# Reordering the half steps of an RWKV-7 scan on one core: partial gram mask, kept state on another engine, low-rank products earlier

## The reference

```python
def step(S, inp):
    r_t, w_t, k_t, v_t, a_t, b_t = inp
    sa = jnp.einsum('zdhij,zdhj->zdhi', S, a_t)
    S = S * w_t[..., None, :] + sa[..., :, None] * b_t[..., None, :] + v_t[..., :, None] * k_t[..., None, :]
    y = jnp.einsum('zdhij,zdhj->zdhi', S, r_t)
    return S, y
```

## Time and profile before

| | us |
|---|---|
| median of three runs | 2652.01 |
| lowest, highest | 2651.32, 2657.9 |
| the profiled execution's own time | 2653.14 |
| its span, first to last instruction | 2650.9 |
| granted TensorE clock over the span | 0.977 |

### The profile page before, as it was taken

The page is one execution under the profiler, slowest core; times in us unless marked ns, Lnnn a source line. Parts: engine busy times, 40 slices in busy tenths (PEclk is TensorE's granted clock), DMA queues, the critical chain, the costliest instruction groups (busy, mean ns, idle before and its releaser), DMA issues. The chain is left out here.

```text
span 2650.9 us, 63375 instructions
## 1 busy us (share of the span) xinstructions
PE 2475.4 (93%) x28048; PEld 2055.0 (78%) x28048; DVE 1259.8 (48%) x2464; ACT 686.7 (26%) x1647; POOL 831.4 (31%) x627
## 2 busy tenths in 40 slices
PE   7999999999998688888888879999999999999997
PEld 6785568888887577777777757878888888888886
DVE  3106650000654456666666656554444444444446
ACT  4115651111111344434434433220011100111002
POOL 3322122222331333324233338023233322433234
PEclk9999999999999799989999989999999999999999
DMA  5100011111110000000000034220011101111014
GB/s 162 44 32 18 2 49 72 72 72 68 37 40 22 37 4 4 4 4 4 3 4 4 4 120 183 89 79 32 33 48 41 40 33 44 37 40 40 33 61 146
DMA packets 39085, 123.09 MB, mean 46 GB/s; under 512 B 11425, under 2 KB 11425, under 8 KB 37665
## 3 DMA queue, kind: packets, MB, share of 16 engines
q1 hardware_dynamic: 38816, 119.06, 12.9%
HBM read 96.24 MB, written 20.97 MB: 44 GB/s over the span
## 5 line engine op out<-in xcount | busy, mean ns | idle before, releaser
L2024 DVE TENSOR_TENSOR ff_f<-ff_f,ff_ps 128x512 f32<-128x512 f32 x300 | 205.5, 687 | 173.6 <-PE ff_ps L98 173.6
L2043 DVE TENSOR_TENSOR ff_sq<-ff_rl 128x512 f32<-128x512 f32 (+1 forms) x96 | 122.4, 1275 | 273.1 <-ACT ff_rl L1941 273.0
L1941 ACT ACTIVATE ff_rl<-ff_ps 128x512 f32<-128x512 f32 (+1 forms) x96 | 50.6, 527 | 754.9 <-PE ff_ps L98 754.9
L733 ACT ACTIVATE sc_xy<-sc_ps 128x256 f32<-128x256 f32 x320 | 120.8, 384 | 225.6 <-PE sc_ps L427 224.1
L1810 POOL TENSOR_TENSOR ff_wd0h<-ff_wdr,params 128x1024 fp32r<-128x1024 f32 x16 | 30.3, 1893 | 458.0 <-DMA ff_wdr<-in_w_down 458.0
L427 PE MATMUL sc_ps<-sc_xy,sc_q 64*64 64x64 f32 x3200 | 166.1, 226 | 0.4 <-issue 0.3
L411 PE MATMUL sc_ps<-sc_xy,sc_ai 64*64 64x64 f32 x3200 | 122.9, 239 | 37.5 <-DVE sc_xy L877 31.4
L977 DVE TENSOR_TENSOR sc_q<-sc_ps,sc_cs 128x128 f32<-128x128 f32 x400 | 98.8, 279 | 122.5 <-PE sc_ps L411 118.8
L423 PE MATMUL sc_ps<-sc_q,sc_xy 64*64 64x64 f32 x2560 | 122.2, 241 | 30.1 <-DVE sc_q L977 24.1
L98 PE MATMUL ff_ps<-hh,ff_wu0h 128*128 128x512 f32 (+1 forms) x384 | 136.7, 356 | 4.4 <-issue 4.4
L427 PEld LDWEIGHTS sc_ps<-sc_xy,sc_q 64*64 64x64 f32 x3200 | 137.8, 142 | 0.7 <-issue 0.5
(11 more groups left out here) (304 smaller groups left out, 7174.8 us busy)
## 6 DMA issues: line engine op xcount, KB each, us to landing
ff_wur<-in_w_up SPq DMA_DIRECT2D x32, 512.0 KB, 3.5
ff_wdr<-in_w_down SPq DMA_DIRECT2D x32, 512.0 KB, 4.2
gwr<-in_w_in SPq DMA_DIRECT2D x31, 512.0 KB, 3.2
gm_dram<-gp_gm SPq DMA_DIRECT2D x8, 1280.0 KB, 4.4
ff_m<-gm_dram SPq DMA_DIRECT2D x16, 640.0 KB, 7.7
fr_x<-in_x SPq DMA_DIRECT2D x10, 512.0 KB, 5.1
ff_xs<-in_x SPq DMA_DIRECT2D x10, 512.0 KB, 3.9
x_dram<-ff_xo SPq DMA_DIRECT2D x10, 512.0 KB, 2.9
```

Of the source, the lines that this page charges most:

```text
L733: nc.scalar.activation(XY[g][:, :, :, :].rearrange("p n u t -> p n (u t)"), yx_out[g], ACT.Copy).then_inc(xy_ready, 1)
L1941: nc.scalar.activation(rl[v % 2][:, 0:tn], ps[:, b, 0:tn], ACT.Relu).then_inc(relu, 1)
L2024: nc.vector.tensor_tensor(own, own, ps[:, 4 + v % 4, :], ALU.add).then_inc(added, 1)
L2043: nc.vector.tensor_tensor(sq[v % 2][:, 0:tn], rl[v % 2][:, 0:tn], rl[v % 2][:, 0:tn], ALU.mult).then_inc(squared, 1)
```

## The change

The edit moves and splits instructions in the four streams; the sums are the same.

- `start_group` masks the strict part first (`begin`, now with the 128 columns of it, signalled by `first_ready`), goes on to the transpose, and masks the other 384 columns last (`mask`). `flip` waits for `masked` of both groups, since it writes into the gram's bank.
- `keep` goes from VectorE to ScalarE, as two passes of 64 columns with a pointer scale.
- In odd half steps `lora_products` stand in front of level 1 and `lora_tanh` behind level 0's copies; the wait for `ta_ready` stands at the first gram. `half` is split over levels 1 and 3, and the two scans go from level 0 of the even half step to level 3 of the odd one. `lora_tanh` waits for the scans of the step before and for POOL's last reading of `icl` (`icl_used`), the scans for the end of POOL's step before (`arr_ready`).
- The second gram stands in front of both level 4 products.
- Both square roots and the products that feed them move back, to between levels 3 and 4.

```diff
@@ POOL, prepare @@
-                own.mark(nc.gpsimd.tensor_tensor(k, fac[:, :, :], both_blocks(raw_k, i), ALU.mult))
-                own.wait()
+                nc.gpsimd.tensor_tensor(k, fac[:, :, :], both_blocks(raw_k, i), ALU.mult).then_inc(icl_used, 1)
+                pool.wait_ge(icl_used, q + 1)
@@ TensorE, flip @@
                 pe.wait_ge(x1_ready, q * GR + g + 1)
+                pe.wait_ge(masked, q * GR + g // HALF * HALF + HALF)
@@ TensorE, side, odd half steps with i == 1 @@
-                    if spot == 0 and ct + 1 < CT:
+                    if spot == 2 and ct > 0:
+                        pe.wait_ge(sqy_ready, ct * NG)
+                        by_head(GRAM_BANK, std, var_ps)
+                    if spot == 2 and ct + 1 < CT:
                         pe.wait_ge(sqk_ready, (ct + 2) * NG)
                         by_head(TOK_BANK, nrm, ss_ps)
-                    if spot == 5 and ct > 0:
-                        pe.wait_ge(sqy_ready, ct * NG)
-                        by_head(GRAM_BANK, std, var_ps)
-                    if spot == 6 and ct > 0:
+                    if spot == 3 and ct > 0:
                         pe.wait_ge(std_ready, ct)
-                    if spot == 1 and ct + 1 < CT:
+                    if spot == 4 and ct + 1 < CT:
                         pe.wait_ge(nrm_ready, ct + 2)
@@ TensorE, the half step @@
                 side(t, 0)
+                if ahead:
+                    lora_products(q + 2)
                 if levels:
                     level_q(q, 1, ga)
...
-                side(t, 6)
+                if ahead:
+                    pe.wait_ge(ta_ready, q + 3)
                 if more:
                     gram_products(qa, sa)
...
                 side(t, 2)
-                if ahead:
-                    lora_products(q + 2)
...
-                if levels:
-                    level_xy(q, 4, ga)
                 side(t, 3)
-                if ahead:
-                    pe.wait_ge(ta_ready, q + 3)
                 if more:
                     gram_products(qa, sb_)
                 if levels:
+                    level_xy(q, 4, ga)
                     level_xy(q, 4, gb)
@@ ScalarE @@
                     if q:
-                        act.wait_ge(arr_ready, q)
+                        act.wait_ge(cum_ready, 2 * q)
+                elif q:
+                    act.wait_ge(icl_used, q)
...
+            def keep(q, g):
+                i, n = q % NB, q * GR + g
+                if fresh(i, 0, g) and fresh(i, 1, g):
+                    return
+                act.wait_ge(s_ready, n)
+                for u in range(2):
+                    last = nc.scalar.activation(kept[:, u, :], S[n % 2][:, u, :], ACT.Copy,
+                                                scale=edge[q % 2][:, g, u:u + 1])
+                last.then_inc(kept_ready, 1)
...
                     level_copy(q, 0, gb)
-                if squares_y and t % 2:
-                    y_square(ct - 1, 1)
-                if t % 2 and i == 1 and ct + 1 < CT:
-                    k_norm(ct + 1, TOK_BANK)
+                if inner:
+                    keep(qs, sa)
+                if ahead:
+                    lora_tanh(q + 2, 0)
+                    lora_tanh(q + 2, 1)
...
                 if squares_y and t % 2:
-                    y_std(ct - 1, GRAM_BANK)
+                    y_square(ct - 1, 1)
...
                     token_copy(qa, sa)
+                if inner:
+                    keep(qs, sb_)
...
                     level_copy(q, 3, gb)
-                if ahead:
-                    lora_tanh(q + 2, 0)
-                    lora_tanh(q + 2, 1)
+                if squares_y and t % 2:
+                    y_std(ct - 1, GRAM_BANK)
+                if t % 2 and i == 1 and ct + 1 < CT:
+                    k_norm(ct + 1, TOK_BANK)
@@ VectorE @@
                 dve.wait_ge(lw_ready, q + 1)
+                if q:
+                    dve.wait_ge(arr_ready, q)
                 nc.vector.tensor_tensor_scan(cum[:, u, way], reset, lw[:, u, way], 0.0,
...
             def mask(q, g):
+                dve.wait_ge(first_ready, q * GR + g + 1)
+                nc.vector.tensor_tensor(GM[g][:, :, 1:4, :], gram_out[:, :, C:4 * C].rearrange("p u (n t) -> p u n t", t=C),
+                                        gmask.rearrange("p (u n t) -> p u n t", u=2, t=C)[:, :, 1:4, :], ALU.mult
+                                        ).then_inc(masked, 1)
+
+            def begin(q, g):
                 n = q * GR + g
                 dve.wait_ge(gram, n + 1)
-                nc.vector.tensor_tensor(GM[g][:, :, :, :].rearrange("p u n t -> p (u n t)"),
-                                        ps[:, GRAM_BANK, :], gmask, ALU.mult).then_inc(masked, 1)
-
-            def begin(q, g):
-                n = q * GR + g
-                dve.wait_ge(masked, n + 1)
+                nc.vector.tensor_tensor(GM[g][:, :, 0, :], gram_out[:, :, 0:C],
+                                        gmask.rearrange("p (u n t) -> p u n t", u=2, t=C)[:, :, 0, :], ALU.mult
+                                        ).then_inc(first_ready, 1)
+                dve.wait_ge(first_ready, n + 1)
...
             def start_group(q, g):
-                mask(q, g)
                 begin(q, g)
                 turn(q, g)
+                mask(q, g)
...
-                    if l == 0 and late:
-                        cumulate(q + 1, 0)
-                        cumulate(q + 1, 1)
...
-                    if l == 3 and inner:
-                        keep(qs, sb_)
+                    if l == 1 and ahead:
+                        half(q + 2, 0)
+                    if l == 3 and ahead:
+                        half(q + 2, 1)
+                        cumulate(q + 2, 0)
+                        cumulate(q + 2, 1)
...
-                if ahead:
-                    half(q + 2, 0)
-                    half(q + 2, 1)
-                if inner and t < PAIRS:
-                    keep(q, ga)
```

21 lines of the change are left out of this document (5 added, 16 removed).

## The result

The change makes the kernel slightly slower. In 20 executions each the medians are 2654.63 us (2649.45 to 2663.31) and 2650.32 before, ratio 1.0022 with a 95% interval of 1.0011 to 1.0032. On another chip the same comparison gave 1.0032 (1.0019 to 1.0045), with 2646.74 before. My forecast was no change, 2651; the time is inside its range, the direction isn't.

The account below looks back on a forecast made before the run. The prediction saw the scan bounded by stops in TensorE's fixed order. Its terms, -7 - 9 - 1 - 8 + 11 - 5.5 + 10 + 12.5 - 4 = -1, took 2652 to 2651 us, range 2643 to 2660.

Parts of the forecast that it names:

- a: Odd half steps: low-rank products in front of level 1 fill the wait for the level copy; 7 us faster.
- b: Odd half steps: the first gram's wait for `lora_tanh` goes entirely; 9 us faster.
- c: Special odd half steps: table load and square roots move to between levels 3 and 4; 1 us faster in all.
- e: Odd half steps: scans at level 3, 2.54 us the pair, delay level 4's joins; 11 us slower.
- f: Even half steps: without scans at level 0, level 1's first product doesn't wait; 5.5 us faster.
- first rival: Scans in odd half steps take 1.48 us because POOL's products come late enough; 2632 us, chance 0.25.
- i: `keep` on ScalarE: two passes taking 0.4 us, hidden, booked 0; 4 us slower if not hidden.
- d: Front of odd half steps: VectorE, without `keep`, reaches the start of the group earlier; 8 us faster.
- h: Middle of even half steps: the side product waits for the remainder mask; 12.5 us slower, lower bound 0.
- g: Front of even half steps: VectorE starts late, meets POOL on `kds`; first product 0.67 later in fifteen, 10 us slower.
- second rival: Even fronts and middles: two POOL holds on VectorE cost 0.6 us more each, plus half clock; 2673 us, chance 0.28.
- j: Clock in the scan: about fourteen half-clock stretches become ten; 4 us faster.

Follow-up runs that it names:

- a0: The changed kernel measured a second time with no edit, against the kernel before: ratio 1.0032 (1.0019 to 1.0045).
- c1: Changed kernel with only the halving that lets POOL start moved to the end of the odd half step: ratio to the kernel before 0.9934.
- a1: Changed kernel with the old mask of 512 columns ahead of the transpose: ratio to the kernel before 0.9959.
- c2: Changed kernel with the halving that lets POOL start moved late and the 512-column mask in every group: 2609.54 us, ratio to the kernel before 0.9859.
- f1: Changed kernel with four first-level products repeated eight times in half steps 6, 16, 26 and 36: ratio to the kernel before 1.0003.

## Why the prediction was wrong

The sum was -1 against a measured +4 to +8, but it came that near by errors that cancel.

- Low-rank products, tanh and specials (a, b, c): booked -17, measured -16 as one lump. That the total is right is in part luck: (b) came as booked, (a) about half, the reciprocals' half steps lost what no term had, and less half clock helped.
- The order of level 4 and the second gram: booked inside (e) as part of an odd half step's 13.5, nothing in even ones. Measured -12 and -13. I followed VectorE's queue there and missed that the gram starts VectorE's chain to the next first product, which gives an even half step 0.24; the shorter stop also went with less half clock.
- Scans (e, f): booked +5.5. Measured -1 and -10, both with the first halving moved too. The 2.54 for the pair was wrong: the scans took 1.27, because they were issued ahead of POOL's L275 and it was L275 that waited. That is the first rival's mechanism, which I gave 0.25.
- `keep` (i, and part of d): booked 0 to -8, measured -3.
- Split mask (d, h): booked +12.5 for the side products, less the share of the 8 in (d). Measured +19 on the kernel before and in the changed one, +11 where the scans are late. The 0.41 at the transpose is real at even fronts (2.42 against 2.83 after the gram), but the remainder in front of the joins takes it all, 0.41 and not the 0.15 that I gave the flips. At an odd front like that of half step 31 it doesn't exist, because POOL's L306 holds VectorE's next instruction past the end of either mask, and on the late-scan base the first product comes 0.1 to 0.4 later. The side products pay 0.6, less than the 0.85; the four groups ahead of the loop 3.5 and more, not booked.
- POOL's start and the even fronts (g): booked +10. The one line that lets POOL start early measured +26 (a0 to c1, a1 to c2). **This is the step that failed.** (g) let the scans make VectorE late at the second group and then meet one instruction of POOL's, on `kds`; and the forecast "books nothing for POOL's earlier start", since POOL still waits for the exponential and the state. It does (rows 2 and the 117.0 above), but L275, L280, L282 and L288 or L291 need neither. VectorE wasn't late; it waited for the gram in all nineteen. But POOL ran on across the end of the odd half step, where in twelve half steps of nineteen L883, L887 and L891 together took 1.8 to 2.9 instead of 0.94. Against c1 the first product comes 16 us later in those twelve, added up, and the loop of the profiled execution has 17 us more at half clock, some 5 by the estimate of 0.3; the remaining 5 aren't placed.
- That (g)'s own number, the first product 0.67 later in fifteen, looks right is luck: over nineteen even fronts it is 11 us later than before, but level 4's place and `keep`, which the sum didn't book there, had first brought it 0.3 sooner (1.89 in c1 against 2.18).
- The mechanism was that of my second rival, two holds that together take over 1.7, at the even fronts alone: its middles have one hold, as before. For the fronts it would have booked 0.67 and 0.6 in fifteen and 6 for the clock, 25 in all, close to the 26. I gave it 0.28.
- Clock (j): booked -4, fourteen stretches going to ten. The two profiled executions did that, 15 in the scan before and 9 after, but the second one of the changed kernel has 13, and the mean clock of all executions fell: 0.976 and 0.974 against 0.980 or 0.981. At 0.3 us lost per us of half clock the difference of 0.005 to 0.007, which is 26 to 37 us of half clock, costs some 8 to 11 us. That is an estimate; it is contained in the figures of the parts above, and without it the change would be a gain of a few us or nothing.

What the parts add up to: c2, which has all of the change but the split mask and POOL's early start, is 37 us faster than the kernel before; the split mask on top costs 20 (c2 to c1) and the early start 26 (c1 to a0), which is +8.5, as a0_again has it. The -37 is measured as a whole. Its parts alone, -16, -12.5 and -3, give -31.5, and the -6 left hold the scans and what the parts do to each other.

## What to carry to other kernels

Letting an engine start as soon as its data allow is not free when it locks out another: ask what runs beside it at its new time, and price that at the place where the next stage waits. Split a step to shorten a chain only where the chain is paced by that step; if something else holds the next instruction anyway, the rest of the split step comes back in front of the next waiting reader. A large regrouping should be tried part by part: here two parts gave 28 us and two others lost 45, and the sum hid it.

## What the runs showed of the hardware

- VectorE's two-input instructions of 0.29 took 0.93, 0.77 (half step 22), 1.18 and 1.31 (half step 26) beside POOL's tensor products and ended 0.14 to 0.15 after them. POOL's L275 took 1.57 beside VectorE's scans, which were issued first, and 0.77 in c1. When POOL issues back to back, two of VectorE's in a row are held. The Trainium skill, page "SBUF — State Buffer", section "Who interferes with whom", says that a VectorE instruction with two SBUF inputs and a GpSimd instruction that reads SBUF exclude each other for a whole instruction, and that issue order decides who waits; these rows agree.
- In the changed kernel the three half steps with the longest stop at the front (first product 3.8 after the start, t = 16, 26, 36) each have 6.8 us at TensorE's 1.2 GHz level. It was costlier than I had read: half step 26 took 17.89 at full clock in f1 and 20.08 with a mean of 0.83 in the changed kernel. Over many executions an us at that level goes with 0.3 us of time. How often it comes differs between executions of one kernel (loop of 624.7 and 631.5 us).
- Moving one group's four level 4 products behind the second gram, without removing any, was worth 0.5% of the whole, part of it through the clock.
